# First strip by pairs of weight rows, merged key norms, earlier one-pass sums in the stick-breaking part: a 1,024-wide two-block transformer in fp32

## The reference, cut to what matters

```python
# block 1
u = rms_norm(h, g_mix) @ w_in                       # 6 x 512 columns: qa, ka, va, qs, ks, vs
qa, ka = partial_rope(qa, cos, sin), partial_rope(ka, cos, sin)   # cos, sin of positions * inv_freq
o = diff_attention(qa, ka, va, lam, g_subln)        # 4 heads; o = rms_norm(o, g_subln) * (1 - lam_init)
# stick-breaking attention, 8 heads
log_1mb = where(strict, log_sigmoid(-z), 0)
between = cumsum(log_1mb, reverse=True) - log_1mb
a = exp(where(strict, log_sigmoid(z) + between, -inf))
h = h + concat([o, a @ v]) @ w_out
h = h + cross_attention(h, mem);  h = h + relu(rms_norm(h) @ w_up)**2 @ w_down
# block 2
proj = rmsnorm(h) @ w_in_2                          # q_a, k_c, v_c, k_s, v_s, k_w, v_w, gates, q_b, k_b, v_b, ...
q_a = rope(rmsnorm(q_a)); k_s = rope(rmsnorm(k_s)); k_w = rope(rmsnorm(k_w))   # 12, 3 and 3 heads of 64
kc = gelu((blocks_of_32_tokens(k_c) + pos) @ w1) @ w2      # 15 blocks, stride 16; w1 is 2048 x 256; vc likewise
# three sparse attentions, a dilated one, gates, w_out, and an MLP follow
```

## Time and profile before

| what | value |
|---|---|
| time, median of 3 runs | 903.5 us (903.1 to 903.57) |
| the profiled execution, own time | 903.28 us |
| its span, first to last instruction | 901.4 us |
| PE busy | 874.8 us, 97% |
| DVE busy | 465.1 us, 52% |
| ACT busy | 426.7 us, 47% |
| POOL busy | 687.4 us, 76% |
| DMA | 149.26 MB, mean 166 GB/s |

### The profile page before, as it was taken

How to read it: one execution, slowest core, us unless ns; L and a number is a source line. 1 busy time by engine, 2 the same in 40 slices (tenths; PEclk the granted TensorE clock), 3 DMA queues, 4 the chain that set the end, 5 groups by cost and what they waited for, 6 DMA issues and landing times.

```text
span 901.4 us, 13249 instructions
## 1 busy us (share of the span) xinstructions
PE 874.8 (97%) x5362; PEld 756.7 (84%) x5362; DVE 465.1 (52%) x663; ACT 426.7 (47%) x582; POOL 687.4 (76%) x395
## 2 busy tenths in 40 slices
PE   7999999999999999999999899999999999999998
PEld 5798876898899999998878788777678899999996
DVE  3578654243335222335787799758964432223333
ACT  4773347446363343333763546346345463443330
POOL 3799357675769999989799588730618979999882
PEclk8999999999999999999999999999999999999999
DMA  8785343344545666655844543620205545565531
GB/s 303 275 279 190 124 140 124 133 141 140 176 148 168 210 200 218 192 193 175 281 150 138 193 124 127 208 95 1 94 1 187 169 145 201 192 224 192 193 131 47
DMA packets 65793, 149.26 MB, mean 166 GB/s; under 512 B 4912, under 2 KB 10192, under 8 KB 65616
## 3 DMA queue, kind: packets, MB, share of 16 engines
q1 hardware_dynamic: 65744, 148.59, 49.2%
HBM read 147.53 MB, written 1.05 MB: 165 GB/s over the span
## 4 chain that ended last, share of the span: by engine, by line
PE 75%; DVE 13%; POOL 4%; ACT 3%; DMA 2%; issue 2%; SPq 0%; DVEq 0%; ACTq 0%
PE ps L1734 65%; POOL w_lo L647 4%; PE ps L1909 2%; DMA raw<-in_w_in 2%; PE ps L1883 2%; PE ps L1821 1%; PE ps L1895 1%; DVE xn L1454 1%; DVE arena L1461 1%; DVE arena L1224 1%; ACT w_hi L687 1%; DVE arena L1456 1%; DVE arena L1094 1%; DMA arena<-in_xT 1%; DVE xn L1623 1%
## 5 line engine op out<-in xcount | busy, mean ns | idle before, releaser
L647 POOL TENSOR_TENSOR w_lo<-raw,w_hi 128x512 fp32r<-128x512 f32 (+2 forms) x370 | 675.6, 1862 | 159.3 <-ACT w_hi L687 151.7
L687 ACT ACTIVATE w_hi<-raw 128x1024 fp32r<-128x1024 f32 (+1 forms) x192 | 247.2, 1326 | 258.1 <-PE ps L1734 134.4
L1734 PE MATMUL ps<-w_hi,x_hi 128*128 128x512 f32 (+1 forms) x672 | 267.8, 399 | 2.4 <-POOL w_lo L647 1.4
L1734 PE MATMUL ps<-w_hi,x_lo 128*128 128x512 f32 (+1 forms) x672 | 261.0, 388 | 0.0
L1734 PE MATMUL ps<-w_lo,x_hi 128*128 128x512 f32 (+1 forms) x672 | 260.8, 388 | 0.0
L1734 PE MATMUL ps<-x_hi,w_hi 128*128 128x256 f32 x704 | 201.5, 286 | 0.6 <-DVE arena L1075 0.6
L1734 PE MATMUL ps<-x_hi,w_lo 128*128 128x256 f32 x704 | 199.2, 283 | 0.0
L1734 PE MATMUL ps<-x_lo,w_hi 128*128 128x256 f32 x704 | 199.2, 283 | 0.0
L1734 PEld LDWEIGHTS ps<-w_hi,x_hi 128*128 128x128 f32 x672 | 126.7, 188 | 35.1 <-issue 7.2
L1734 PEld LDWEIGHTS ps<-w_hi,x_lo 128*128 128x128 f32 x672 | 126.5, 188 | 26.5
L1734 PEld LDWEIGHTS ps<-w_lo,x_hi 128*128 128x128 f32 x672 | 126.9, 189 | 23.1
(11 more groups left out here) (270 smaller groups left out, 824.1 us busy)
## 6 DMA issues: line engine op xcount, KB each, us to landing
raw<-in_w_in SPq DMA_DIRECT2D x35, 1024.0 KB, 5.2
raw<-in_w_up SPq DMA_DIRECT2D x32, 1024.0 KB, 5.3
raw<-in_w_down SPq DMA_DIRECT2D x32, 1024.0 KB, 4.8
raw<-in_w_xkv SPq DMA_DIRECT2D x8, 1024.0 KB, 5.0
raw<-in_w_out SPq DMA_DIRECT2D x8, 1024.0 KB, 4.9
raw<-in_w_xq SPq DMA_DIRECT2D x4, 1024.0 KB, 5.2
raw<-in_w_xo SPq DMA_DIRECT2D x4, 1024.0 KB, 4.9
raw<-in_w_o_a SPq DMA_DIRECT2D x3, 1024.0 KB, 4.8
```

The costliest lines, as they stand in the source:

```text
L647: x = nc.gpsimd.tensor_tensor(LO[s % 2][:, 2048 * q + d0:2048 * q + d1], RAW[n % 3][:, d0:d1], HI[s % 2][:, 2048 * q + d0:2048 * q + d1].b ...
L687: nc.scalar.activation(HI[s % 2][:, 2048 * q + c0:2048 * q + c1], RAW[n % 3][:, c0:c1], ACT.Copy).then_inc(hi_done, 1)
L1734: last = T.matmul(dst, l, r, start=start and i == 0, stop=stop and i == 2, skip_group_check=w_stationary)
```

## The change

**First strip.** Halves 0, 1 and 2 are loaded in two pieces each (`raw_part` for the first), strip 0's high parts are made by quarters, and VectorE makes all four low parts (`lo_part`), as well as the second quarter of the first half of strips 1 and 2 (`LO_SHARED`). TensorE takes the 8 weight rows in groups of two rows, the three products interleaved. x's rows are issued after half 3, the constants and the rotary inputs after half 4. VectorE computes the angles after evacuating strips 0 and 1 (the move of that block is not in the cut below); ScalarE computes the sine between the halves of strip 3. Strip 2 writes to banks 4 and 5.

**Stick-breaking part.** The first half's sums are made as one-pass products of high and low parts with fp32r copies of the triangle and the -1 block (`tri2`). The squares are taken ahead of the halves. `g_subln` is one value per partition (its loads' elements lie one on each), applied as a scale in the copies after the transposes. The first token tile is transposed before strip 9's second part, which is now one call. The high parts of strips 9 and 10 are issued earlier in ScalarE's queue.

**Block 2's keys.** `key_norms` does both norms at once; `head_tables(2)` comes ahead of strip IN2+4's low parts; `u2_evac(4)` comes after the hidden row's copy; the patches are stored once, in groups that the w1 products read without stride (`kcg`).

```diff
-gsub = small(128)
+gsub = small(1)
...
+def pieces(s, q, size):
+    return [(0, size // 2), (size // 2, size)] if q == 0 or s < 2 else [(0, size)]
...
-    return n + 1 - (n >= 1) - (n >= RAW_W1)
+    return n - 1 - (n >= RAW_W1)
+LO_SHARED = {1: 5, 2: 6}
...
+        d["pair"] = 4 if s == 2 else 0 if 6 <= s <= 9 or IN2 + 11 <= s < IN2 + 13 else 2 * (turn % 2)
...
-TABLES_AT = {IN2: (0, 1), IN2 + 5: (2,), IN2 + 7: (3, 4)}
+TABLES_AT = {IN2: (0, 1), IN2 + 4: (2,), IN2 + 7: (3, 4)}
...
-    misc.append((gsub, a["g_subln"][0].partition_broadcast(P)))
+    misc.append((gsub, a["g_subln"][0].rearrange("(p o) -> p o", o=1)))
...
         if n >= 3:
-            if n - 3 < 2:
-                sp.wait_ge(lo_first, n - 2)
-            if n - 3 == 0:
-                sp.wait_ge(lo_done, 1)
-            elif n - 3 == 1:
-                pass
+            if n in (3, 4):
+                sp.wait_ge(lo_first, 2 * (n - 2))
...
                 sp.wait_ge(lo_done, los(n - 3))
+            if n in (5, 7):
+                sp.wait_ge(lo_first, 5 if n == 5 else 6)
...
-        if n == 0:
-            sp.dma_start(dst[:, 0:2, :], src[:, 0:2, :]).then_inc(raw_first, 16)
-            sp.dma_start(xT[:, 1024:2048], a["xT"][:, 1024:2048]).then_inc(xT_loaded[1], 16)
+        if n < 3:
+            sp.dma_start(dst[:, 0:2, :], src[:, 0:2, :]).then_inc(raw_part[n], 16)
...
         sp.dma_start(dst, src).then_inc(raw_loaded[n % 3], 16)
-        if n == 2:
+        if n == 0:
+            sp.dma_start(xT[:, 1024:2048], a["xT"][:, 1024:2048]).then_inc(xT_loaded[1], 16)
+        if n == 3:
             sp.dma_start(h[:, :, :], a["x"].rearrange("o (t p) d -> p (o t) d", p=P)).then_inc(x_loaded, 16)
+        if n == 4:
...
         for q, n in enumerate(half_of[s]):
-            if s == 0 and q == 1:
+            parts = pieces(s, q, halves[n][1])
+            if s == 0:
                 continue
-            parts = pieces(q, halves[n][1])[:1 if s == 0 else 2]
+            if q == 0 and s in LO_SHARED:
+                parts = parts[:1]
...
+                pool.wait_ge(hi_done, HI_COUNT[s, q, i])
...
-            raw_wait(act, n)
-            for c0, c1 in pieces(q, halves[n][1]):
+            for i, (c0, c1) in enumerate(pieces(s, q, halves[n][1])):
+                if i == 0 and n == 2:
+                    act.wait_ge(raw_part[2], 16)
+                else:
+                    raw_wait(act, n)
...
     split(0, xT, 0)
-    act.wait_ge(raw_first, 16)
-    nc.scalar.activation(HI[0][:, 0:1024], RAW[0][:, 0:1024], ACT.Copy).then_inc(hi_done, 1)
+    def first_hi(n, i):
+        if i == 0:
+            act.wait_ge(raw_part[n], 16)
+        else:
+            raw_wait(act, n)
+        nc.scalar.activation(HI[0][:, 2048 * n + 1024 * i:2048 * n + 1024 * i + 1024],
+                             RAW[n][:, 1024 * i:1024 * i + 1024], ACT.Copy).then_inc(hi_done, 1)
+    first_hi(0, 0)
+    first_hi(0, 1)
...
     split(0, xT, 4)
-    raw_wait(act, 0)
-    raw_wait(act, 0)
-    nc.scalar.activation(HI[0][:, 1024:2048], RAW[0][:, 1024:2048], ACT.Copy).then_inc(hi_done, 1)
-    raw_wait(act, 1)
-    nc.scalar.activation(HI[0][:, 2048:4096], RAW[1][:, 0:2048], ACT.Copy).then_inc(hi_done, 1)
+    first_hi(1, 0)
+    first_hi(1, 1)
...
     norm_stats(0, h)
-    act.wait_ge(lam_arg, 1)
-    nc.scalar.activation(lame, lams, ACT.Exp).then_inc(lam_exp, 1)
     hi(2)
+    hi(3, 0)
...
     nc.scalar.activation(scs, ang, ACT.Sin).then_inc(rope_sin, 1)
...
+    hi(3, 1)
...
     norm_stats(1, memx)
+    act.wait_ge(lam_arg, 1)
...
+    def ya_to_hi(t):
+        act.wait_ge(ya_done, t + 1)
+        nc.scalar.activation(ya_cols(XH, t), ya_tile, ACT.Copy, scale=gsub).then_inc(ya_hi, 1)
+    hi(9)
...
             link(nc.scalar.activation(wide(sbz[j % 2]), z_bank(j), ACT.Abs))
+        if half == 1:
+            ya_to_hi(0)
...
+        if half == 0:
+            for j in js:
+                act.wait_ge(z_sp, j + 1)
+                nc.scalar.activation(XH[0][:, 768 * j:768 * j + 768], sbz[j], ACT.Copy).then_inc(z_hi, 1)
...
+        else:
+            ya_to_hi(1)
...
-        if half == 1:
+        if half == 0:
+            hi(10)
+        else:
             sb_to_hi(1)
-        hi(10 + half)
+            hi(11)
...
     hi(IN2 + 4)
-    hi(IN2 + 5)
...
     head_squares(1, KS, 3)
-    head_roots(1, 3)
     head_squares(2, KW, 3)
-    head_roots(2, 3)
+    hi(IN2 + 5, 0)
+    head_roots(2, 6, 2)
+    hi(IN2 + 5, 1)
...
-    for loaded in xT_loaded:
...
+    def lo_part(s, q, i):
+        c0 = 2048 * q + 1024 * i
+        n = 2 * s + q
+        dve.wait_ge(hi_done, HI_COUNT[s, q, i])
+        V.tensor_tensor(LO[s % 2][:, c0:c0 + 1024], RAW[n % 3][:, 1024 * i:1024 * i + 1024],
+                        HI[s % 2][:, c0:c0 + 1024].bitcast(f32), ALU.subtract).then_inc(lo_first, 1)
...
-    for n_hi, raw, c0, c1 in ((2, 0, 1024, 2048), (3, 1, 2048, 4096)):
-        dve.wait_ge(hi_done, n_hi)
-        V.tensor_tensor(LO[0][:, c0:c1], RAW[raw][:, c0 - 2048 * raw:c1 - 2048 * raw],
-                        HI[0][:, c0:c1].bitcast(f32), ALU.subtract).then_inc(lo_first, 1)
+    lo_part(0, 0, 0)
+    lo_part(0, 0, 1)
+    dve.wait_ge(xT_loaded[1], 16)
+    split_x(0, xT, 4, 8)
+    lo_part(0, 1, 0)
+    lo_part(0, 1, 1)
+    lo_part(1, 0, 1)
+    row_scale(0)
+    evac(0, u_qa, rows=rstd_n[:, 0:2])
+    lo_part(2, 0, 1)
+    evac(1, u_ka, rows=rstd_n[:, 0:2])
...
-    row_scale(0)
-    evac(0, u_qa, rows=rstd_n[:, 0:2])
...
-    broadcast_rstd(0, bank(4))
+    broadcast_rstd(0, bank(6))
...
     unit_loop(0, U_X, post_diff, hook_diff, early_diff)
+    V.tensor_copy(tri2, cst[:, C_TRI:C_TRI + 256]).then_inc(tri_ready, 1)
+    ya = xn[:, :, 0:512]
+    link(V.tensor_tensor(sq1.rearrange("p (t c) -> p t c", t=NT), ya, ya, ALU.mult))
+    V.tensor_reduce(ss_s, sq1.rearrange("p (s c) -> p s c", c=P), AX.X, ALU.add).then_inc(sub_sq, 1)
...
-        link(V.tensor_tensor(yv, yv, bc(rv.unsqueeze(3), [P, NT, 4, P]), ALU.mult))
-        link(V.tensor_tensor(yv, yv, bc(gsub.unsqueeze(1).unsqueeze(1), [P, NT, 4, P]), ALU.mult))
+        V.tensor_tensor(yv, yv, bc(rv.unsqueeze(3), [P, NT, 4, P]), ALU.mult).then_inc(ya_ready, 1)
+    def ya_to_lo(t):
+        dve.wait_ge(ya_hi, t + 1)
+        V.scalar_tensor_tensor(ya_cols(XL, t), ya_tile, gsub, ya_cols(XH, t).bitcast(f32),
+                               ALU.mult, ALU.subtract).then_inc(ya_lo, 1)
...
             sb_to_lo(0)
+            ya_to_lo(0)
...
         if half == 0:
+            for j in range(2):
+                dve.wait_ge(z_hi, j + 1)
+                c = slice(768 * j, 768 * j + 768)
+                V.tensor_tensor(XL[0][:, c], sbz[j], XH[0][:, c].bitcast(f32), ALU.subtract).then_inc(z_lo, 1)
...
+            ya_to_lo(1)
...
+    def key_norms():
+        dve.wait_ge(tables_ready, 3)
...
+        va = ta.rearrange("p (a c) -> p a c", c=384)[:, 0:4:3, :]
...
+        dve.wait_ge(hn_sq, 3)
+        V.tensor_reduce(ss_h[:, 0:12], vb.rearrange("p (s c) -> p s c", c=HD), AX.X, ALU.add).then_inc(hn_ss, 2)
...
+        dve.wait_ge(hn_y0, 3)
+        newton(rs_h[:, 0:12], ss_h[:, 0:12], y0_h[:, 0:12], HD)
...
+            r = rs_h[:, 6 * b:6 * b + 6].rearrange("p (t m) -> p t m", t=NT).unsqueeze(3)
+            for o in dup_views(kdup[b]):
+                V.tensor_tensor(o, a4, bc(r, [P, NT, 3, HD]), ALU.mult).then_inc(dve_step, 1)
...
+    V.tensor_copy(kcg[:, :, 0:2], src[:, 0:16].rearrange("p (b w) -> p w b", b=2))
...
+            dst = kcg[:, :, c:c + 32 * n].rearrange("p w (i r) -> p i w r", r=32)[:, :, :, 0:16]
+            for z in range(2):
+                last = V.tensor_copy(dst[64 * z:64 * z + 64], src[64 * x:64 * x + 64, :, :, :, z])
...
-    head_norm(1, KS, 3, dup_views(kdup[0]))
-    head_norm(2, KW, 3, dup_views(kdup[1]))
-    u2_evac(4)
+    key_norms()
...
     signal(kc_ready, 1)
+    u2_evac(4)
...
+            if s in LO_SHARED:
+                pe.wait_ge(lo_first, LO_SHARED[s])
...
+        xs = {"h": xh, "l": xl}
+        ws = {"h": hi_, "l": lo_}
+        order = [("hh", 0), ("lh", 0), ("hh", 2), ("lh", 2), ("hl", 0), ("hl", 2),
+                 ("hh", 4), ("lh", 4), ("hh", 6), ("lh", 6), ("hl", 4), ("hl", 6)]
+        for (x, w), k0 in order:
+            if w == "h":
+                pe.wait_ge(hi_done, 1 + k0 // 2)
+            else:
+                pe.wait_ge(lo_first, 1 + k0 // 2)
+            pe.wait_ge(split_hi if x == "h" else split_lo, k0 + 2)
+            for k in (k0, k0 + 1):
+                for o in range(NT):
+                    last = T.matmul(bank(d["pair"] + o), xs[x][:, S * k + P * o:S * k + P * o + P],
+                                    ws[w][:, 512 * k:512 * k + 512], start=x + w == "hh" and k == 0,
+                                    stop=x + w == "hl" and k == 7, skip_group_check=True)
...
     def z_sums(j):
-        pe.wait_ge(z_sp, j + 1)
...
+        b = z_bank(j)
+        if j < 2:
...
+            c = 768 * j
```

(26 more changed lines are left out.)

121 lines of the change are left out of this document (51 added, 70 removed).

## The result

The changed kernel takes 891.11 us (median of 4, 890.34 to 891.23), the kernel before on the same chip 903.3 us. The ratio is 0.9863, 95% interval 0.9846 to 0.988: faster by 12.2 us where 12.1 were forecast. The profiled execution took 891.22 us, its span is 889.2 us.

A forecast was written before the change was run, and what follows sets the result against it. TensorE, busy 97% of the span, was taken to bound the kernel. Terms 6.0 + 3.1 + 3.0 = 12.1 us off 903.28 gave 891.2, 891.4 with the median's 0.2; range 886 to 898.

The forecast's parts named there:

- First strip: Kernel start: TensorE's groups never wait, 8.05 to 19.0 at full clock, 7.3 us earlier; strip 1 ends at 29.9.
- The new wait: Strip 3's middle: angles, slowed beside GpSimd's chunks, ready at 41.6, hold the sine and low part; TensorE stalls 2.0 us.
- the 43 and the 4.7 us: Start, if the port pair locks exclusively: 8 chunks take longer, angles come at about 43, gain 4.7 instead of 6.0.
- The start's 6.0: Start up to strip 4: begins at 58.0 instead of 64.0, 6.0 us gained; 8.2 without the wait in strip 3.
- Stick-breaking's 3.1: Stick-breaking part: one-pass sums save 1.1 us and the y transposes' idle goes, 3.1 us, range 1 to 3.5.
- the wait of 1.80: Stick-breaking, y transposes: TensorE's 1.80 us idle for VectorE's low part, 1.96 from issue to issue, was to go.
- The keys' 3.0: Second block's keys: 2.70 us wait and half clock go (4.4), 1.4 lost to the table; 3.0 us, -1 to 5.
- (1): Rival, start: VectorE's angles come without being held; gain 14.3, time 889.2 us; chance 0.17.
- (2): Rival, strip 3 or IN2+4: stalls grow and the clock falls once or twice, 1.7 each; 894 to 897 us; chance 0.22.
- (3): Rival, stick-breaking and keys: these two later parts give nothing; 897.5 us; chance 0.10.
- (4): Rival, start: quarters land late, groups stall as the passes did, later losses eat the rest; no difference; chance 0.04.
- (5): Rival, start: rotary inputs land late and the sine holds ScalarE's queue; slower if landing is beyond 51.2; chance 0.04.

The follow-up runs named there:

- the start alone: Only the first strip's part of the change (pieces, VectorE's low parts, groups, load order, sine and angles) on the kernel before: 896.26 us, ratio 0.992.
- The run with the copies late: Changed kernel with the first y tile's two copies back directly ahead of the second tile's: 893.41 us, ratio 0.9885 to before printed as 0.9886.

## Why the prediction was right, and where it was not

**First strip.** Right: 11.0 us at full clock, ending at 19.4 (forecast 19.0), and strip 1 at 30.3 (29.9). Both are late by the 0.36 us by which the first matmul is (8.42 for 8.06).

**The new wait.** Right in its place and cause: the angles were ready at 42.6 (41.6), TensorE stood 1.51 us in strip 3 (2.0). The Trainium skill, SBUF — State Buffer, rules on the shared port pair, has the pair as an exclusive lock for a whole instruction; GpSimd's 8 chunks took 10.03 us beside eight of VectorE's short steps, 1.25 each, so the stretching that I weighed by that rule is not there, and only VectorE paid. That the 43 and the 4.7 us worked out with it lie so near to what was measured (42.6 and 4.74) is luck: the lateness has another source, the next paragraph's.

**The start's 6.0.** This term was too large by 1.3 us (4.74; 5.22 with the start alone). The step that failed was GpSimd's run of 8 chunks from 30.2 to 40.5: I followed only the first half of strip 2's weights. The second half landed at 29.9, ScalarE's high part came behind it,

```profile
29.93 1.92 ACT L702 ACTIVATE w_hi<-raw 128x2048 fp32r<-128x2048 f32 x1 [2.20 <-DMA raw<-in_w_in]
```

and the run lasted from 31.92 to 41.95. So the angles came 1.0 us late, strip 3's second half began at 50.05 instead of 49.0, and the transposes ended at 59.0 instead of 58.0; 0.36 of this last 1.0 us is the late first matmul. For the same reason TensorE waited 0.67 us in strip 2, which ended at 42.6 instead of 41.1, but that didn't reach strip 4, since strip 3's second half had to wait for GpSimd in any case. Last, 0.3 us more are gone between strip 4 and the second mark, which I did not trace.

**Stick-breaking's 3.1.** Measured 3.32, and in the same size alone. Eight one-pass pairs take 0.28 us each (128.93 to 131.17), where 0.29 was taken; the wait of 1.80 is gone. The run with the copies late shows that their place made it. The multiply by g_subln, which the working counted as what makes y ready early, gave nothing by itself: y is ready 6 us ahead.

**The keys' 3.0.** Alone 2.96: the 2.70 and the slow clock gone, 1.31 us of wait for the table added (1.4 forecast). In the changed kernel it is 4.06, since the 0.77 us wait, which the sum left in place, goes with the shift. That and the start's miss nearly cancel; that the total came out to 0.3 us is in part luck.

**The rivals.** (1), the angles not held: excluded by the 1.2 us steps. (2), the clock falls at the new waits: not in the changed kernel; in three of the experiments it did, at 1.64, 2.16 and 2.69 us of wait in the first 60 us. (3) and (4): excluded by the marks. (5), a late landing of the rotary inputs: they had landed by 31.8, where VectorE did not wait for them.

## What to carry to other kernels

An early gain on the bounding engine is only worth what the chains behind it let through: the groups were worth 3.6 us at the first strip's end and 0.7 to 1.2 three strips later, and the next 2.2 us at that place came with moving the short serial steps of another engine to where its neighbour rests. When instructions of two engines shut each other out, count the short ones at the neighbour's chunk length, wherever they fall beside a run of chunks. Add up parts by marks in the trace: here three parts apart gave 13.5 us and together 12.1, and two of them changed a stretch that they do not touch by 0.9 and 1.5 us.
